# The fetched tokens' rows of h2: transposed from the unsplit h2 at the head of the query stage, and kept on chip

## What is computed

```python
def peer(h, w_pq, sub_k1, sub_k2, u_tab, v_tab):      # h = h2, the normalised input
    def blk(xb):
        q = (xb @ w_pq).reshape(PEER_BLOCK, PEER_HEADS, PEER_DKEY)
        s1 = einsum('thd,nd->thn', q[..., :half], sub_k1)
        s2 = einsum('thd,nd->thn', q[..., half:], sub_k2)
        v1, i1 = lax.top_k(s1, PEER_TOPK)
        v2, i2 = lax.top_k(s2, PEER_TOPK)
        ...                                           # top 16 of the 256 sums, idx, g = softmax
        ue = u_tab[idx]
        ve = v_tab[idx]
        a = jnp.einsum('td,thkd->thk', xb, ue)
        wgt = g * jax.nn.gelu(a, approximate=False)
        return jnp.einsum('thk,thkd->td', wgt, ve)
```

## Time and profile before

| what | us |
|---|---|
| median of 3 runs | 3962.49 |
| lowest and highest | 3959.23, 3965.61 |
| span of the profiled execution | 3965.6 |
| TensorE busy | 3818.9 |
| VectorE busy | 3049.1 |
| GpSimd busy | 1318.5 |
| ScalarE busy | 1099.4 |

### The profile page before, as it was taken

The page is one execution under the profiler, slowest core; times in us unless marked ns, Lnnn a source line. Parts: engine busy times, 40 slices in busy tenths (PEclk is TensorE's granted clock), DMA queues, the critical chain, the costliest instruction groups (busy, mean ns, idle before and its releaser), DMA issues.

```text
span 3965.6 us, 67094 instructions
## 1 busy us (share of the span) xinstructions
PE 3818.9 (96%) x24995; PEld 3757.7 (95%) x24995; DVE 3049.1 (77%) x3858; ACT 1099.4 (28%) x1126; POOL 1318.5 (33%) x923
## 2 busy tenths in 40 slices
PE   8999999999989998999999999999999999999999
PEld 7989999999889998999999999999999999999999
DVE  6887888788855445388859999998678888888876
ACT  3323233232222112222233333332222222222222
POOL 3333333333334342454532222222133323333320
PEclk9999999999999999999999999999999999999999
DMA  7789888887878998799979999999888989888895
GB/s 275 262 313 325 289 281 299 320 301 265 308 260 284 319 380 308 264 372 369 353 251 385 387 383 383 389 379 390 314 313 340 353 321 343 342 329 337 338 350 189
DMA packets 451684, 1285.17 MB, mean 324 GB/s; under 512 B 34368, under 2 KB 258368, under 8 KB 343360
## 3 DMA queue, kind: packets, MB, share of 16 engines
q1 hardware_dynamic: 372576, 876.99, 62.1%
q0 software_dynamic: 46080, 335.56, 21.5%
q10 hardware_dynamic: 32832, 70.07, 4.6%
HBM read 1070.18 MB, written 345.75 MB: 357 GB/s over the span
## 4 chain that ended last, share of the span: by engine, by line
PE 42%; issue 32%; POOL 14%; DMA 7%; DVE 3%; ACT 1%; POOLq 0%; SPq 0%; DVEq 0%; ACTq 0%
PE ST L1951 19%; PE ST L1859 17%; POOL w_lo L654 14%; DMA w_raw<-w_all 4%; PE PA L1859 3%; PE ST L1927 2%; DMA rows<-v_rows,v_idx 2%; DVE w_lo L1009 1%; ACT w_hi L717 1%; DVE PA L1518 1%; DMA rows<-u_rows,v_idx 1%; PE PA L1841 1%; PE ST L1874 0%; DMA u_rows<-u_out 0%; POOL w_lo L646 0%
## 5 line engine op out<-in xcount | busy, mean ns | idle before, releaser
L654 POOL TENSOR_TENSOR w_lo<-w_raw,w_hi 128x512 fp32r<-128x512 f32 x588 | 793.3, 1381 | 1218.1 <-ACT w_hi L717 1184.6
L717 ACT ACTIVATE w_hi<-w_raw 128x2048 fp32r<-128x2048 f32 x368 | 703.7, 1913 | 1334.5 <-PE ST L1951 513.2
L1951 PE MATMUL ST<-wt_hi,w_hi 128*128 128x384 f32 x2048 | 686.5, 335 | 13.9 <-DVE w_lo L1009 13.7
L1951 PE MATMUL ST<-wt_hi,w_lo 128*128 128x384 f32 x2048 | 684.5, 334 | 0.0
L1951 PE MATMUL ST<-wt_lo,w_hi 128*128 128x384 f32 x2048 | 684.3, 334 | 0.0
L1009 DVE TENSOR_TENSOR w_lo<-w_raw,w_hi 128x2048 fp32r<-128x2048 f32 x219 | 501.1, 2288 | 206.5 <-ACT w_hi L717 199.2
L690 POOL DMA_INDIRECT rows<-v_rows,v_idx x160 | 323.2, 2020 | 736.0 <-DVE PA L1518 667.0
L1619 PE MATMUL PA<-h_hi,w_hi 128*128 128x272 f32 x2496 | 541.1, 298 | 3.8 <-DVE w_lo L1009 3.8
L1619 PE MATMUL PA<-h_hi,w_lo 128*128 128x272 f32 x2496 | 521.7, 291 | 0.0
L1619 PE MATMUL PA<-h_lo,w_hi 128*128 128x272 f32 x2496 | 520.2, 290 | 0.0
L1859 PE MATMUL ST<-h_hi,w_hi 128*128 128x384 f32 x1408 | 508.8, 361 | 2.2 <-ACT h_b L917 1.6
(11 more groups left out here) (272 smaller groups left out, 6241.9 us busy)
## 6 DMA issues: line engine op xcount, KB each, us to landing
w_raw<-w_all SPq DMA_DIRECT2D x368, 1024.0 KB, 7.5
u_in<-w_all SPq DMA_DIRECT2D x128, 1024.0 KB, 8.6
u_rows<-u_out SPq DMA_DIRECT2D x512, 256.0 KB, 7.4
v_rows<-w_all SPq DMA_DIRECT2D x128, 1024.0 KB, 10.3
a_scr<-gb ACTq DMA_DIRECT2D x128, 192.0 KB, 6.3
g_scr<-g_st ACTq DMA_DIRECT2D x24, 1024.0 KB, 11.3
gl_st<-g_scr SPq DMA_DIRECT2D x30, 768.0 KB, 10.6
a_st<-a_scr SPq DMA_DIRECT2D x30, 768.0 KB, 13.2
```

Of the source, the lines that this page charges most:

```text
L654: ins = pool.tensor_tensor(w_lo[:, slot, cols], raw[:, slot, cols], w_hi[:, slot, cols].bitcast(F32), ALU.subtract)
L717: act.activation(w_hi[:, slot, :], raw[:, slot, :], ACT.Copy).then_inc(hi_ready, 1)
L1951: last = mm(PB[n % 2][:, k, :], a, r_[b][:, c, :], start=(c == 0 and y == 0), stop=(c == GRP - 1 and y == 2))
```

## The change

On TensorE a new `h2_turn(k)` transposes tile k of `h2_s`, unsplit fp32, twice: the 128 tokens into ST bank 0 or 1, the 32 tokens into bank 2 or 3, four k to a bank, alternating. It stands one k ahead of the products of the head. VectorE may write `h2_lo[k]` over `h2_s[k]` only behind `h2t_ready` of k. ScalarE's `rows_of_bank(b)` copies two filled banks, reordered, to `rows2` (the third row buffer, free until the fetches begin) and to `h2_b`, at k = 5, 9, 13 and at the end, and there issues the three DMAs that spread `h2_b`. ScalarE's wait for the stores of x2 moves ahead of the head. At the turn the identity matmuls, their copies and their waits are gone; ScalarE makes one copy of `rows2` into `h2_g`, behind the last unit of the choices stage, and raises `h2g_ready`, for which VectorE's loop and the fetch of slot 2 wait.

```diff
@@ GpSimd
             for j in range(SLOTS):
+                if j == 2:
+                    pool.wait_ge(h2g_ready, 1)
                 fetch(j)
@@ ScalarE, head of the query stage
             for s in u_stored:
                 act.wait_ge(s, 64 * NKEY // 2 + 1)
+            for s in x2_stored:
+                act.wait_ge(s, 16 * NO // 2 + 1)
+            def rows_of_bank(b):
+                act.wait_ge(h2t_ready, 4 * b + 4)
+                for dst, w, bank in ((rows2_q, P, b % 2), (h2_b, BT, 2 + b % 2)):
+                    act.activation(dst[0:w, :, P * b:P * (b + 1)].rearrange("p q (k j) -> p q k j", j=32),
+                                   ST[0:w, bank, :].rearrange("p (k q j) -> p q k j", q=4, j=32), ACT.Copy)\
+                        .then_inc(h2t_taken, 1)
             for k in range(KD):
                 act.wait_ge(h2_scaled, k + 1)
                 act.activation(h2_hi[:, k, :], h2_s[:, k, :], ACT.Copy).then_inc(h2_rounded, 1)
+                if k > 4 and k % 4 == 1:
+                    rows_of_bank(k // 4 - 1)
+            rows_of_bank(KD // 4 - 1)
+            act.wait_ge(h2t_taken, KD // 2)
+            for g in range(1, BG):
+                act.dma_start(h2_b[g * BT:(g + 1) * BT, :, :], h2_b[0:BT, :, :]).then_inc(h2b_spread, 16)
@@ ScalarE, turn (h2_ordered, its calls and the three DMAs are removed)
+            act.activation(h2_g, rows2[:, :], ACT.Copy).then_inc(h2g_ready, 1)
+            for n in range(2):
+                u_slot(TT * TOPK_UNITS // 2, n, PD)
@@ VectorE
                     dve.wait_ge(h2_rounded, k)
+                    dve.wait_ge(h2t_ready, k)
                     V.tensor_tensor(h2_lo[:, k - 1, :], h2_s[:, k - 1, :], h2_hi[:, k - 1, :].bitcast(F32), ALU.subtract)\
...
-            dve.wait_ge(h2t_taken, 16)
+            dve.wait_ge(h2g_ready, 1)
@@ TensorE, head of the query stage
+            def h2_turn(k):
+                pe.wait_ge(h2_scaled, k + 1)
+                if k == 0:
+                    pe.wait_ge(ostd_ready, 1)
+                elif k >= 8 and k % 4 == 0:
+                    pe.wait_ge(h2t_taken, k // 2 - 2)
+                b, c = k // 4 % 2, slice(k % 4 * P, (k % 4 + 1) * P)
+                nc.tensor.transpose(ST[:, b, c], h2_s[:, k, A0:T], ident)
+                nc.tensor.transpose(ST[0:BT, 2 + b, c], h2_s[:, k, B0:A0], ident).then_inc(h2t_ready, 1)
+            h2_turn(0)
...
             for k in range(KD):
+                if k + 1 < KD:
+                    h2_turn(k + 1)
                 pe.wait_ge(h2_ready, k + 1)
...
             pe.wait_ge(late_loaded, 32)
+            pe.wait_ge(h2t_taken, KD // 2)
@@ TensorE, turn (h2_turned is removed)
-            u_unit(TT * TOPK_UNITS // 2, 0, PD, {KD // 2: lambda: h2_turned(0), KD - 1: lambda: h2_turned(1)})
-            u_unit(TT * TOPK_UNITS // 2, 1, PD, {KD // 2 + 1: lambda: h2_turned(2), KD - 1: lambda: h2_turned(3)})
-            pe.wait_ge(h2t_taken, 16)
+            for n in range(2):
+                u_unit(TT * TOPK_UNITS // 2, n, PD)
```

More of the change, by code:

```diff
@@ L269, in build @@
         h2_bg = h2_b[:, :, :].rearrange("p a n -> p (a n)")
+        rows2_q = rows2[:, :].rearrange("p (a n) -> p a n", a=4)
         PV = [p[:, :, 0:HT] for p in pair]
@@ L344, in build @@
         o_loaded = sem("o_loaded")
-        h2t_ready, h2t_taken, a_g_ready = sem("h2t_ready"), sem("h2t_taken"), sem("a_g_ready")
+        h2t_ready, h2t_taken, h2g_ready, a_g_ready = sem("h2t_ready"), sem("h2t_taken"), sem("h2g_ready"), sem("a_g_ready")
         acc_g_ready, acc_g_turned, acc_g_added = sem("acc_g_ready"), sem("acc_g_turned"), sem("acc_g_added")
@@ L882, in _ @@
                     hi(v + (U_PQ // 2 + 1), n)
-            for s in x2_stored:
-                act.wait_ge(s, 16 * NO // 2 + 1)
             def u_slot(v, n, src):
@@ L1862, in u_unit @@
                 last.then_inc(unit_done, 1)
[L1864 to L1876, removed]
             for tt in range(TT):
```

## The result

The changed kernel takes 3976.49 us, the median of seven runs (3973.74 to 3981.09). The kernel before, run beside it, takes 3962.49 (seven runs, 3958.58 to 3970.09). The ratio is 1.0035, with a 95% interval of 1.0025 to 1.0045: **slower by 14 us**, where 18.5 us less was forecast. The profiled execution has a span of 3979.3 us. Two executions of the experiments ran in a slower state and took 7034.9 us (e1) and 14816.4 us (e4); e4's median is 3945.36 us without it and 3948.03 with it.

What follows compares the result with a forecast made beforehand. TensorE, busy 96% of the span, was taken as the bound. Turn -22.6, head +3.3 and ScalarE +0.75 gave -18.5 us, from a median of 3962.5 to 3944 us, range 3938 to 3951; the forecast had chance 0.80.

Steps and rivals of the forecast that it cites:

- What bounds the kernel: TensorE, busy 96% of the span; a removed matmul is worth its time wherever TensorE never waits, if neighbours keep up.
- The turn: Between units 40 and 42 of peer_u: removing identity matmuls and waits saves 22.8 us, net -22.6 us.
- +0.2 for w_lo: At the turn, GpSimd's w_lo of unit 42 was expected to make TensorE wait 0.2 us.
- (2): At the first gate matmul: the one-hots are ready with ten us to spare, so TensorE's wait for them does not return.
- (3): VectorE's dot-product loop after the turn: fetched row 0 comes some 3 us late for VectorE, with nothing of it on TensorE.
- The head: Head of the query stage: 14 pairs of transposes at 0.22 us, plus 0.2 at the low clock, add 3.3 us.
- ScalarE's issues: Behind the head, ScalarE's last bank copies and three DMA issues delay w_hi, w_lo and TensorE by 0.75 us.
- The rule against it: In the head, by the skill's 275 ns each, not counted for the clock, 28 transposes would cost 7.7 us, not 3.1.
- The rivals: Low clock in head (3963 us, 0.05), gate-loop give-back (3951, 0.08), lock-step (3982, 0.03), one-hot wait returning (3947.5, 0.04).
- Lock-step: In the head, VectorE's answer to each transpose falls behind the product and TensorE stands each k: +38 us, 3982; chance 0.03.
- given back in the gate loop: Late row fetches and w_lo come out on TensorE in the gate loop, costing 7 us: 3951; chance 0.08.
- what is gained should travel on: With TensorE fully busy and VectorE 92% in the later gate loop, the turn's gain should last beyond it.

Runs made afterwards that it cites:

- e1: The changed kernel with 189 idle semaphore increments at the start of TensorE's program: 3951.96 us, 0.997 of the kernel before.
- e4: The changed kernel with TensorE's peer_v loop written out, no branch back: 3945.36 us, 0.9967 of the kernel before.
- e7: e5 plus the change's turn alone, without transposes, rows2 and h2_b filled with constants: 3940.05 us, 25.5 us below e5.
- e8: e4 with the first two w_hi of the query stage ahead of ScalarE's three DMA issues: 3944.70 us, 0.9968 of the kernel before.
- e2: The kernel before with 67 idle semaphore increments at TensorE's start, loop at 179 as in the changed kernel: 3995.60 us, 1.0088 of before.
- e10: The changed kernel with 20 idle semaphore increments at TensorE's start, loop at 199: 3986.28 us, 1.006 of the kernel before.
- e3: The changed kernel with 40 idle semaphore increments at TensorE's start, loop at 219: 3948.61 us, 0.997 of the kernel before.
- e11: The changed kernel with e3's 40 increments and e8's later DMA issues, peer_v loop kept: 3941.41 us, 0.9945 of the kernel before.
- e5: The kernel before with TensorE's peer_v loop written out: 3965.53 us, 1.0022 of the kernel before.
- e6: e5 plus the change's head part alone (transposes, bank copies, DMAs), the turn done as before: 3974.27 us, 8.7 us above e5.

## Why the prediction was wrong, point by point

- **What bounds the kernel.** Right: TensorE, and a removed matmul gives its time where it stands.
- **The turn: -22.8, +0.2 for w_lo.** Right: 23.1 us in the stage, 25.5 as a time of its own (e7). The term for GpSimd's w_lo was not needed, since no wait is listed there. The one-hots did not become late, as (2) says. The rows of the fetch did keep VectorE waiting, as (3) says, for 24.5 us in the whole gate loop and not 3, and still without a cost on TensorE.
- **The head: +3.3.** Right in size: 14 pairs at 0.22 us, the clock as assumed. The low clock took the first product, as before. The measured stage, +3.3, holds the next term as well, so the sum of both was too high by 0.75. That is within the noise of a stage, which is up to 1.8 us wide here.
- **ScalarE's issues: +0.75.** Right for the wait, slightly small: the wait for w_lo grew by 0.95 us and fell back by 1.0 with the issues moved (e8). The terms as written, 1568.6 + 1.2 + 1.9, end at 1571.7 and not at 1571.9, so they give 0.55. That the wait comes out whole in the stage is not shown (e8).
- **The rule against it.** The Trainium skill, TensorE: Matmul & The Clock Gate, Part 4, has transposes not counting as work for the clock and one at about 275 ns. The second agrees with the length of the rows here, 0.27 us; the mistake was to take it as a price, since the next one starts 0.11 us later. The first is not tested: the clock stayed at 1.00, but two transposes are only 0.22 us of each 1.72.
- **The rivals.** None came true. Lock-step would have shown as waits for h2_lo: there is one of 0.2 us. The gain was not given back in the gate loop, where 0.6 us at most came out.
- **The step that failed** is the sentence "what is gained should travel on", and the sum built on it, which has no term for anything behind the gate loop. I took the stages behind the turn as unchanged because no instruction of theirs is. But the change also makes TensorE's program shorter by 189 instructions, and that moves every loop behind it against the blocks in which code is fetched. It cost 33.8 us in the rounds of peer_v: -18.5 + 33.8 = +15.3, where +14.0 was measured. That the two agree to 1.3 us is in part luck: the same slow branches cost 29.8 us in the rounds of e2 and about 40 in those of e10. What could have been seen in advance: a loop on the bounding engine, a count of its body (1572) near a number of whole blocks, the packets of q8, and a changed count ahead of it. What could not: at which places it falls out, since no trace of before showed it. With the 35 places in 256 counted since, it deserved a chance of about one in seven as a rival of its own, with a price that this profile did not hold.

**Open.** e3 is 13.2 us below before and e11 21.6, and their edits differ by 1 us of one wait. e5 is some 7 us above the kernel before, and e6 4.5 above what the head stage says. So builds of almost the same kernel differ by up to 0.2% for reasons that no row here shows, which is more than each run's own interval; peer_v's waits for w_lo add up to anything between 7.1 and 14.5 us in these traces and may be part of it. It doesn't touch the main point, which is shown from both sides; its size is less certain. By differences to before it is 33.8 us in e2, 27 from the change to e3 (+14.0 and -13.2) and 36 from e10 to e3 (+23.2 and -13.2). Why the second wait comes eleven matmuls behind the first, and which blocks the nine packets are, is open.

## What to carry to other kernels

An edit moves the code behind it, and where the bounding engine runs a long loop, count the body and its place before and after: with the body of 1572 instructions here, twenty instructions ahead of it decided over 10 us at every branch back (144.0 against 133.7 us a round). Other lengths of body were not tried. If a result comes out on the wrong side while every edited stage is as forecast, compare the sequencer's branch row and the packets of the instruction queue, and shift the program by some tens of idle instructions before doubting the edit. DMA issues take time on an engine that others wait for: three took 1.9 us here and made one wait of TensorE 1.0 us longer. Look at the stage before counting such a wait as a loss, since here its removal did not shorten it.

## What the runs showed of the hardware

- A branch back on TensorE over the same body of 1572 instructions takes 0.21 us at some places of the loop and 5.7 us at others. The second case costs 7 to 10 us a round (141.4, 142.4 and 144.0 us against 133.7 to 134.1), of which 5.5 to 8.1 (22.0 / 4 in e2, 23.0 / 4 in the change, 32.4 / 4 in e10) are waits of TensorE; part of the rest is the lower granted clock behind them, 0.67 in the stretch shown.
- The branch was cheap with the loop at 112, 152 and 219 (by the remainder of 256) and dear at 179 and 199, with 36 packets of q8 more for four branches. That seven blocks of 256 stay and eight do not fits this, and is not seen directly.
- 189 semaphore increments in a row take 0.15 us each on TensorE, three times the 51 ns of their rows. Forty of them at the start were hidden behind its first wait.
- fp32 transposes of 128x128 and 32x128 between fp32r matmuls cost 0.11 us each, by the distance between starts, at a granted clock of 1.00; their rows last 0.27 us.
